# A transformer trunk in one kernel: rows of h 400 words long, gating one pair behind the products, and one interruption of the weight stream per attention unit

## What is computed

```python
def trunk_layer(x, cond, lp, l, ctx_cache):
    mod = jax.nn.silu(cond) @ lp['w_ada'] + lp['b_ada']
    ...
    h = rmsnorm(x, lp['norm_ffn1']) * (1 + sc1) + sh1
    x = x + 0.5 * g1 * swiglu(h, lp['ffn1_w1'], lp['ffn1_w3'], lp['ffn1_w2'])
    h = rmsnorm(x, lp['norm_mix']) * (1 + sc2) + sh2
    mix, ctx_out = token_mixing(h, lp, l, ctx_cache)
    x = x + g2 * mix
    h = rmsnorm(x, lp['norm_ffn2']) * (1 + sc3) + sh3
    x = x + 0.5 * g3 * swiglu(h, lp['ffn2_w1'], lp['ffn2_w3'], lp['ffn2_w2'])
    return x, ctx_out
```

## Time and profile before

| | us |
|---|---|
| median of 3 runs | 2159.68 |
| lowest and highest | 2153.47, 2161.18 |
| the profiled execution | 2152.92 |
| its span in the trace | 2151.1 |

### The profile page before, as it was taken

One profiled execution on the slowest core, in us unless ns is written; L12 is line 12 of the kernel. 1 busy time (PEld: TensorE's weight loads), 2 busy tenths in 40 slices (PEclk: granted clock), 3 DMA queues, 4 the chain that ended last, 5 costly groups with the idle time before them and its releaser, 6 DMA issues.

```text
span 2151.1 us, 30049 instructions
## 1 busy us (share of the span) xinstructions
PE 2029.4 (94%) x10992; PEld 1898.5 (88%) x10992; DVE 1492.9 (69%) x2460; ACT 785.2 (37%) x1291; POOL 448.2 (21%) x357
## 2 busy tenths in 40 slices
PE   6999997999899999999999999989988999999998
PEld 6999996877668999999999999878766799999998
DVE  7889898556564467878888788975657544684544
ACT  4323235333343253333443333542333523533333
POOL 2302023211124521010130000221121353210101
PEclk9999998999999999999999999989999999999999
DMA  7776663222122335656556556522211223454332
GB/s 307 251 230 230 217 202 128 71 91 66 59 72 84 100 126 187 201 189 205 178 208 197 177 182 195 168 95 80 79 63 61 74 86 103 165 160 135 127 117 88
DMA packets 82539, 309.55 MB, mean 144 GB/s; under 512 B 9428, under 2 KB 10890, under 8 KB 81536
## 3 DMA queue, kind: packets, MB, share of 16 engines
...
## 4 chain that ended last, share of the span: by engine, by line
PE 62%; DVE 25%; ACT 6%; issue 6%; DMA 0%; POOL 0%; ACTq 0%; SPq 0%; DVEq 0%; POOLq 0%
PE bank L1424 51%; DVE lo L830 5%; DVE areaM L1028 4%; DVE areaO L1028 3%; ACT hi L563 3%; PE ps_br L1424 2%; PE ps_s L1664 2%; PE ps_o L1690 2%; DVE tiny L1199 1%; DVE areaF L1005 1%; DVE areaF L1002 1%; ACT pr L758 1%; DVE areaF L997 1%; DVE areaG L1251 1%; DVE x L1037 1%
## 5 line engine op out<-in xcount | busy, mean ns | idle before, releaser
L1424 PE MATMUL bank<-h_hi,hi 128*128 128x384 f32 (+1 forms) x2272 | 801.4, 353 | 17.5 <-POOL h_lo L1326 6.9
L1424 PE MATMUL bank<-h_hi,lo 128*128 128x384 f32 (+1 forms) x2272 | 773.2, 340 | 0.0
L1424 PE MATMUL bank<-h_lo,hi 128*128 128x384 f32 (+1 forms) x2272 | 772.8, 340 | 0.0
L830 DVE TENSOR_TENSOR lo<-raw,hi 128x1024 fp32r<-128x1024 f32 (+1 forms) x396 | 485.8, 1227 | 252.1 <-ACT hi L563 250.9
L563 ACT ACTIVATE hi<-raw 128x1024 fp32r<-128x1024 f32 (+1 forms) x396 | 430.3, 1087 | 308.9 <-PE bank L1424 306.3
L1424 PEld LDWEIGHTS bank<-h_hi,hi 128*128 128x128 f32 x2272 | 431.0, 190 | 71.7 <-issue 48.9
L1424 PEld LDWEIGHTS bank<-h_lo,hi 128*128 128x128 f32 x2272 | 431.8, 190 | 1.4
L1424 PEld LDWEIGHTS bank<-h_hi,lo 128*128 128x128 f32 x2272 | 431.9, 190 | 0.0
L1424 PE MATMUL bank<-g_hi,hi 128*128 128x384 f32 x832 | 283.8, 341 | 24.3 <-ACT areaF L645 12.8
L1303 POOL TENSOR_TENSOR g_lo<-areaF,g_hi 128x384 f32 x88 | 107.0, 1217 | 894.3 <-ACT g_hi L654 703.3
L1424 PE MATMUL bank<-g_hi,lo 128*128 128x384 f32 x832 | 282.6, 340 | 0.0
(11 more groups left out here) (232 smaller groups left out, 1849.2 us busy)
## 6 DMA issues: line engine op xcount, KB each, us to landing
raw<-w_main SPq DMA_DIRECT2D x332, 512.0 KB, 4.0
...
```

What stands on the lines that cost most here:

```text
L830: dve.tensor_tensor(lo[:, slot, 0:w], raw[:, slot, 0:w], hi[:, slot, 0:w].bitcast(F32), ALU.subtract).then_inc(lo_ready, 1)
L1424: last = pe.matmul(dst, wt[:, slot, w], ac[:, c, 0:cols], start=c == 0 and k == 0, stop=c == chunks - 1 and k == 2)
```

## The change

Rows of h_hi and h_lo become 400 words. In `up` ScalarE's and VectorE's work on a pair is moved: the SiLU comes at the odd tile, the gating (`gate_up`) after the drain of the next pair's even tile, and the copy to g_hi behind that, on ScalarE in all phases. For q = 0 the second product on VectorE falls away. `down` takes all but the last two chunks of its first two tiles, then those two chunks of both. In the mixing, `attention_steps` lays the values of unit u - 2, the transposes of unit u - 1 and the scores of unit u next to each other, and runs SWA and DF on as one row of 24 units. The second score of a DF unit stands one number later. The sine MLP's two steps are further apart, pairs of filter, spectrum and convolution steps stand together, the sums of subnorm are taken by two matmuls of 64 rows, and the modulation shares shift a little. Loops of ScalarE and TensorE in the feed forward are written out.

```diff
-FILTER_TILES = 13
-NA_EARLY = 3
+H_PITCH = T + 16
+FILTER_TILES = 14
+NA_EARLY = 2
...
-ADA_SHARE = {(0, 0): (10, 6, 13, 6, 10, 3), (0, 1): (8, 5, 9, 5, 8, 2), (1, 0): (8, 4, 8, 4, 8, 3), (1, 1): (8, 0, 0, 0, 0, 0)}
+ADA_SHARE = {(0, 0): (12, 5, 13, 6, 10, 2), (0, 1): (8, 6, 9, 6, 8, 0), (1, 0): (8, 5, 9, 5, 8, 0), (1, 1): (8, 0, 0, 0, 0, 0)}
...
-def attention_steps(kind):
+def attention_steps(*kinds):
+    units = [(kind, u) for kind in kinds for u in range(12)]
     out = []
-    if kind == DF:
-        out += [("scores", kind, 0, 0), 1.3, ("scores", kind, 0, 1), ("probs", kind, 0), 1.5]
-        for u in range(12):
-            if u + 1 < 12:
-                out.append(("scores", kind, u + 1, 0))
-            if u < 6:
-                out.append(("short", u))
-            if 7 <= u < 7 + TB:
-                out.append(("subinv", 0, u - 7))
-            if u == 7 + TB:
-                out.append(("subout", 0))
-            out += [0.9, ("turn", kind, u), 0.9, ("values", kind, u), 0.1]
-            if u + 1 < 12:
-                out += [("scores", kind, u + 1, 1), ("probs", kind, u + 1)]
-            out.append(1.5)
+    for at in range(len(units) + 2):
+        if at >= 2:
+            kind, u = units[at - 2]
+            out.append(("values", kind, u))
             if u % 6 == 5:
-                out += [("square", u // 6), 0.6, ("subnorm", u // 6)]
-        return out + [0.8] + [("subinv", 1, b) for b in range(TB)] + [0.6, ("subout", 1), 0.2]
-    out += [("scores", kind, 0, 0), ("probs", kind, 0), 1.5]
-    for u in range(12):
-        if u + 1 < 12:
-            out.append(("scores", kind, u + 1, 0))
-        out += [1.0, ("turn", kind, u)]
-        if u + 1 < 12:
-            out.append(("probs", kind, u + 1))
-        out += [1.2, ("values", kind, u), 0.2]
-        if u % 6 == 5:
-            out.append(("outs", kind, u // 6))
+                out.append(("square", u // 6) if kind == DF else ("outs", kind, u // 6))
+        if 1 <= at <= len(units):
+            out.append(("turn", *units[at - 1]))
+        if at == len(units):
+            out.append(2.0)
+            continue
+        if at > len(units):
+            break
+        kind, u = units[at]
+        out.append(("scores", kind, u, 0))
+        if kind != DF:
+            out += [1.0, ("probs", kind, u), 1.0]
+            continue
+        out += [1.0, ("scores", kind, u, 1)]
+        if u == 7:
+            out.append(("subnorm", 0))
+        if u < 6:
+            out.append(("short", u))
+        if 8 <= u < 8 + TB:
+            out.append(("subinv", 0, u - 8))
+        if u == 8 + TB:
+            out.append(("subout", 0))
+        out += [1.0, ("probs", kind, u), 1.0]
+    if DF in kinds:
+        out += [0.6, ("subnorm", 1), 0.8] + [("subinv", 1, b) for b in range(TB)] + [0.6, ("subout", 1), 0.2]
     return out
...
-        if s[0] == "turn" or s[0] in ("proj", "out") and s[-1] == 1:
+        if s[0] == "probs" or s[0] in ("proj", "out") and s[-1] == 1:
             flush(fed)
...
-    fil = [1.0, ("sinmlp", 0), 1.5, ("sinmlp", 1), 4.5]
+    fil = [0.5, ("sinmlp", 0), 5.0, ("sinmlp", 1), 5.5]
     for o in range(2):
         for tk in range(TB):
-            fil += [("taps", o, tk), 3.3, ("tapsum", o, tk), 0.3]
-        fil += [("scale", o), 3.0]
-        for fc in range(TB):
-            fil += [("filter", o, fc), 0.8]
+            fil += [("taps", o, tk), 3.5, ("tapsum", o, tk)]
+        fil += [0.3, ("scale", o), 3.0, ("filter", o, 0), ("filter", o, 1), 1.6, ("filter", o, 2), 0.8]
...
-        if turns and isinstance(s, tuple) and s[0] == "values":
-            rest += [0.5, turns.pop(0), 0.3]
+        if turns and isinstance(s, tuple) and (s[0], turns[0][0]) in (("probs", "vk"), ("scores", "rope")):
+            rest += [0.5, turns.pop(0)] if s[0] == "probs" else [turns.pop(0)]
...
-    swa, df = attention_steps(SWA), attention_steps(DF)
+    plan += paced(gate_parts[:until], both)
-        hy += [("ytok", o, 0), 1.2, ("ytok", o, 1), 1.5]
-        for fc in range(TB):
-            hy += [("spectrum", o, fc), 0.8]
-        hy += [1.0, ("conv", o, 0), 0.8, ("conv", o, 1), 2.0]
+        hy += [("ytok", o, 0), 1.2, ("ytok", o, 1), 1.5, ("spectrum", o, 0), ("spectrum", o, 1), 1.6, ("spectrum", o, 2), 1.8,
+               ("conv", o, 0), ("conv", o, 1), 2.8]
...
-        h_hi, h_lo = sb("h_hi", [P, C, T + 2], F32R), sb("h_lo", [P, C, T + 2], F32R)
+        h_hi, h_lo = sb("h_hi", [P, C, H_PITCH], F32R), sb("h_lo", [P, C, H_PITCH], F32R)
...
+                def high(i):
+                    if p.q:
+                        act.wait_ge(gf_ready, fcount(p) + i - FB + 1)
+                    else:
+                        act.wait_ge(drained, p.n0 + 2 * i + 2)
+                    act.activation(g_hi[:, i, :], gf[:, i % 2, 0:T], ACT.Copy).then_inc(g_hi_ready, 1)
+                for j in range(p.tiles):
+                    n, i, s = p.n0 + j, j // 2, j // 2 % 2
+                    if j or not p.first:
+                        split(n + AHEAD)
+                    if p.q == 0 and j % 2 == 0:
+                        if i:
+                            high(i - 1)
+                        act.wait_ge(tile_done, n + 1)
+                        if fcount(p) + i >= 2:
+                            act.wait_ge(drained, n - 2)
+                        act.activation(sil[:, s, 0:T], bank[n % RING][:, 0:T], ACT.Silu).then_inc(silu_done, 1)
+                    elif p.q and j % 2:
+                        act.wait_ge(drained, n)
                         for g, (t0, t1) in enumerate(GROUPS):
                             last = act.activation(sil[:, s, t0:t1], sil[:, s, t0:t1], ACT.Silu, bias=sil[:, s, T + g:T + g + 1])
                         last.then_inc(silu_done, 1)
...
+                        if i:
+                            high(i - 1)
...
+                high(THIRDS[p.third] - 1)
...
                         dve.wait_ge(tile_done, n + 1)
-                        dve.tensor_tensor(sil[:, s, :], b[:, 0:T + 2], rstd_one, ALU.mult).then_inc(scaled_ready, 1)
+                        if f - FB >= 2:
+                            dve.wait_ge(gf_ready, f - FB - 1)
+                        dve.tensor_tensor(sil[:, s, :], b[:, 0:T + 2], rstd_one, ALU.mult).then_inc(drained, 1)
+                        if j:
+                            gate_up(p, f - 1)
...
+                        dve.tensor_tensor(gf[:, s, :], b[:, 0:T + 2], rstd_one, ALU.mult).then_inc(drained, 1)
...
+                        dve.tensor_tensor(gf[:, s, 0:T], sil[:, s, 0:T], b[:, 0:T], ALU.mult).then_inc(drained, 2)
                     modulations(n)
+                if p.q:
+                    gate_up(p, fcount(p) + THIRDS[p.third] - 1)
+            def gate_up(p, f):
+                i = f - fcount(p)
+                s = i % 2
+                dve.wait_ge(silu_done, f + 1)
+                dve.wait_ge(drained, p.n0 + 2 * i + 2)
+                for g, (t0, t1) in enumerate(GROUPS):
+                    last = dve.scalar_tensor_tensor(gf[:, s, t0:t1], gf[:, s, t0:t1], gf[:, s, T + g:T + g + 1], sil[:, s, t0:t1],
+                                                    ALU.add, ALU.mult)
+                last.then_inc(gf_ready, 1)
...
                 for j in range(C):
-                    split(p.n0 + j + AHEAD)
+                    if raw is None or j < C - 1:
+                        split(p.n0 + j + AHEAD)
                     add_to_x(p.n0 + j, j)
                     if raw is not None:
                         raw_after(raw, j)
+                        if j == C - 1:
+                            split(p.n0 + j + AHEAD)
                     modulations(p.n0 + j)
...
-                        pool.wait_ge(drained, n + 1 + 4 * i)
+                        pool.wait_ge(g_hi_ready, f + 1 + 2 * i)
...
                 pe.wait_ge(silu_done, f + THIRDS[p.third])
+                k = THIRDS[p.third]
+                early, late = range(k - 2), range(k - 2, k)
+                for chunks in (early, late):
+                    for j in range(2):
+                        if chunks is early:
+                            ready(p.n0 + j)
+                        tile(p.n0 + j, g_hi, g_lo, k, T, None if j else product, only=chunks)
+                for j in range(2, C):
+                    ready(p.n0 + j)
+                    tile(p.n0 + j, g_hi, g_lo, k, T)
...
-                        pe.matmul(ps_t[:, 0:T], bones, sub_n, start=True, stop=True).then_inc(t_ready, 1)
+                        for a in (0, 64):
+                            last = pe.matmul(ps_t[a:a + 64, 0:T], ones[a:a + 64, a:a + 64], sub_n[a:a + 64, :], start=True, stop=True)
+                        last.then_inc(t_ready, 1)
```

57 lines of the change are left out of this document (5 added, 52 removed).

## The result

| | before | after |
|---|---|---|
| median of 4 runs, us | 2157.70 | 2171.01 |
| lowest and highest | 2153.47, 2161.18 | 2167.40, 2172.49 |
| the profiled execution | 2152.92 | 2167.40 |
| its span | 2151.1 | 2165.6 |

The changed kernel takes 1.006 times as long as before (95% interval 1.0036 to 1.0084). It is slower by 13 us, where 2107 us and a gain were forecast. The kernel before has one run more here than in the table ahead of the prediction, which moves its median from 2159.68 to 2157.70 us.

What follows compares the result with a forecast made beforehand. TensorE's stream, busy for 94% of the span, was taken as the bound. Terms 10 + 20 + 1 + 18 - 4 + 6 + 2 = 53 us gave 2107 us for the median, range 2072 to 2135.

Steps and rivals of the forecast that it cites:

- The attentions: Attention units of both layers: new step order removes 40.6 us of waits, 25 come back; 18 us saved, from 0 to 40.
- rival (d): Attentions: VectorE's chain so long that late transposes hold up the scores, slower at 2179 us; chance 0.05.
- (b): Attentions: VectorE's scaling late for all 72 units, so the 18 us do not come, 2125 us; chance 0.12.
- Rows of h: Matmuls reading h in mixing and ups: rows of 400 words bring g's pace; 10 us saved, from 0 to 15.
- rival (a): Rows of h: the pitch does nothing, the paces come from something other than the row's start, 2117 us; chance 0.15.
- Up to down: Change from up to down: SiLU wait goes and g_lo waits shrink, 20 us saved; later split ending down adds 1.
- The end of DF: Last DF values to the branch's product: longer wait for o_lo and half matmuls of subnorm, a loss of 4 us.
- the sine MLP: Second step of the sine MLP in the mixing: five parts ahead instead of two, 6 us saved for both layers.

Runs made afterwards that it cites:

- e17: Changed kernel with POOL making only the last 128 of a low half's 1280 columns and VectorE 1152 instead of 640; 2145.89 us.
- e5: Changed kernel with the transposes of a DF pair one number of the list later, between first and second score; 2134.15 us.
- e10: e5 with 1.6 instead of 1.0 ahead of DF's transposes, 0.4 ahead of the probabilities, and the short term behind them; 2142.36 us.
- e2: Kernel before with only the changed list of the mixing; 2208.18 us.
- e3: Changed kernel with rows of h of 386 words again; 2170.68 us.
- e7: Changed kernel with the old list of the mixing and h's rows read with 384 columns stored 384 words apart; 2122.56 us.
- e8: Changed kernel with DF's old list and h's rows read with 384 columns stored 384 words apart; 2109.69 us.
- e9: Changed kernel with DF's old list and TensorE's old order of chunks in the downs; 2133.00 us.
- e11: Changed kernel with the six short terms moved from DF's units to SWA's, behind the probabilities; 2162.15 us.

## Why the prediction was wrong, step by step

**The attentions: the step that failed.** The forecast was that 40.6 us of waits go, 25 come back, and 18 are gained. In place of that the mixings lost 49. The mechanism was rival (d)'s, a late transpose in front of the next score, with waits mis-sized and the clock left out. I took DF units with a short term 1.4 and 0.9 us late, SWA 3 us a layer; the transposes of one layer waited 23.5 us, up to 3.5. By the prediction's own sign (b)'s condition was met as well, since NA's and SWA's transposes waited 16.6 us. Three things were missing from the working. First, what else stands ahead of the scaling in VectorE's queue, as a short term does: in the units of subnorm operations of 0.94 and 0.62 us, and a branch's gating of 0.55. Second, the scaling was taken at 1.67 us, from a unit in which its last step took 0.62; beside POOL it takes 3.5 (658.85 to 662.36). Third, and the largest, the waits were costed one by one at full clock. The waits of the transposes, with 0.17 for each, came to 47.1 + 34 x 0.17 = 52.9 us where 25 were put. That is 28 / 72 = 0.39 us for each unit above what I took, under the 0.74 from which (d) was to begin. By the waits alone the kernel would still have been some 25 us faster (an estimate, 53 - 28). The 37 us of busy time turned it round. The reading of the waits also had a gap: the 3.2 us of DF's transposes were not among those at stake.

**The clock.** In the attentions the sum held it at 0.99. The idle time of layer 0 rose by only 6.3 us, and busy time by 18.7. This term was absent from the attentions' part of the sum, and e17's two layers show it apart from the rest. The total of the waits doesn't foretell it, as the mixings of layers 0 and 1 show in e5 (first two rows) and e10:

```profile
351.30:767.60 416.30, 384.23 (x1961) 324.28 (x1961) 230.94 (x438) 143.57 (x278) 116.82 (x92) 0.97 0.24 80
1382.30:1804.70 422.40, 390.87 (x1960) 328.45 (x1961) 232.32 (x438) 143.52 (x278) 116.14 (x92) 0.95 0.23 79
```
```profile
354.60:780.60 426.00, 395.07 (x1961) 333.66 (x1961) 232.90 (x438) 143.56 (x278) 118.61 (x92) 0.94 0.24 78
1396.80:1815.30 418.50, 386.04 (x1961) 326.86 (x1961) 232.72 (x438) 143.59 (x278) 118.53 (x92) 0.97 0.24 80
```

In layer 0 e10 idles 30.9 us and e5 32.1, yet e10 is busy for 10.8 us more; in layer 1 it is busy for 4.8 us less, with 32.5 us idle against 31.5. Part of this is not the list's at all. Up to the end of NA in layer 0 the changed kernel and e5 have the same instructions, and still NA took 67.0 us in the one and 71.0 in the other, with 5.8 and 5.5 us idle:

```profile
428.60:495.60 67.00, 61.17 (x322) 47.95 (x320) 38.95 (x83) 24.10 (x54) 9.79 (x9) 1.00 0.28 87
```
```profile
427.80:498.80 71.00, 65.47 (x322) 51.24 (x321) 37.67 (x83) 24.09 (x54) 10.40 (x9) 0.93 0.25 82
```

A difference of some 4 us in one stage of one trace can thus be the clock alone. The 37 us are far above that, they stand in both layers, and e2 has them in the kernel before too (mixings of 439.3 and 436.9 us at 0.93 and 0.94). That the clock is the larger part of the loss is shown. Which wait lets it fall and which doesn't isn't settled.

**Rows of h.** A gain of 10 us was forecast and none measured (e3), so rival (a) held for the time. Its reason, that the pace comes from something else than the row's start, did not: the distance of the rows changes the pace in e7. "g's rows are a multiple of 16 words" was the wrong reading: what g's rows and e7's have in common is a row of 1536 bytes. At that pace e8 gained 5.4 us between medians whose runs overlap, and 5.5 were counted for 384 columns; e7 at the same pace gained nothing, so that the price came out near is no more than luck.

**Up to down.** Right in kind, too small: 34.6 us outside the mixings against 20 + 1. No wait for the SiLU is left, as forecast. The 4.4 us put to g_lo in last thirds became 1.0; the working had the products behind the last drain at their longest, and whether that is the reason wasn't looked at. e9 gives 18 us to the chunks, which leaves some 16 for the rest. More than the 20 us of waits in the earlier trace rows went; which of the shorter gaps make up the difference wasn't taken apart.

**The end of DF and the sine MLP.** The wait for o_lo stayed at 3.3 us, where 2.4 more were forecast. The sine MLP waits 6.6 us instead of 13.3, as forecast (6 saved).

**The range** ended at 2135, and (d) had a chance of 0.05. Its argument against (d) was that only half of the DF units have a short term in the chain. e11 shows that the chain is too long without one.
